# Query and key preparation inside the input projection, squares of each norm one stage earlier, setup and first adaptive vectors in one stage

## The reference, cut to what matters

```
for l in range(DEPTH):
    sh1, sc1, gt1, sh2, sc2, gt2 = adaln_vectors(cvec, W['ada_w'][l], W['ada_b'][l])
    h = modulate(rms_norm(x, W['norm1_w'][l]), sh1, sc1)
    # l == 0: even_mixer(h, ...); l == 1: odd_mixer(h, ...)
    x = x + gt1 * y
    h = modulate(rms_norm(x, W['norm2_w'][l]), sh2, sc2)
    x = x + gt2 * sq_relu_mlp(h, W['mlp_w1'][l], W['mlp_w2'][l])
```

```
qa, ka, va, qb, fa, fb, vb, gb = jnp.split(h @ w_in, offs, axis=-1)
qa = rms_norm(qa.reshape(bsz, n_tok, A_HEADS, HEAD_DIM), q_norm)
ka = rms_norm(ka.reshape(bsz, n_tok, A_KV_HEADS, HEAD_DIM), k_norm)
# latent tokens: qa, ka = apply_rope(...); then block_attention
q = jax.nn.silu(heads_b(qb, B_DK))
f_f = lb + (1 - lb) * jax.nn.sigmoid(heads_b(fa, B_DK))
o = rms_norm(o_f + o_b[:, ::-1], g_norm) * jax.nn.silu(heads_b(gb, B_DV))
```

## Time and profile before

| | us |
|---|---|
| median of 3 runs | 2501.28 (2498.02 to 2506.66) |
| profiled execution | 2492.64 |
| its span, first to last instruction | 2490.8 |
| PE busy | 2208.8 (89%) |
| DVE busy | 1125.0 (45%) |
| ACT busy | 839.3 (34%) |
| POOL busy | 279.0 (11%) |

### The profile page before, as it was taken

The page is one execution under the profiler, slowest core; times in us unless marked ns, Lnnn a source line. Parts: engine busy times, 40 slices in busy tenths (PEclk is TensorE's granted clock), DMA queues, the critical chain, the costliest instruction groups (busy, mean ns, idle before and its releaser), DMA issues. The chain is left out here.

```text
span 2490.8 us, 58690 instructions
## 1 busy us (share of the span) xinstructions
PE 2208.8 (89%) x26275; PEld 1882.8 (76%) x26275; DVE 1125.0 (45%) x2028; ACT 839.3 (34%) x1513; POOL 279.0 (11%) x526
## 2 busy tenths in 40 slices
PE   5999676879899999988996888888888789999999
PEld 2588354548799999974585677777776669999998
DVE  0311365533543244218133677777784354324421
ACT  3222355431421122126222565556653232111211
POOL 0000032100000000000000444343442000000000
PEclk9999798889899999999998899999998899999999
DMA  6110003881122222202110000000000212322221
GB/s 247 68 68 34 13 1 134 312 309 32 54 83 68 85 68 79 74 18 76 68 68 5 8 7 9 9 9 9 9 6 5 102 51 68 85 68 73 80 69 59
DMA packets 160742, 167.75 MB, mean 67 GB/s; under 512 B 13788, under 2 KB 117996, under 8 KB 160364
## 3 DMA queue, kind: packets, MB, share of 16 engines
q1 hardware_dynamic: 160492, 164.00, 20.4%
HBM read 160.44 MB, written 3.54 MB: 66 GB/s over the span
## 5 line engine op out<-in xcount | busy, mean ns | idle before, releaser
L168 PE MATMUL psum<-arena 64*64 64x64 f32 (+6 forms) x17072 | 828.9, 248 | 158.1 <-DVE arena L1033 17.7
L168 PEld LDWEIGHTS psum<-arena 64*64 64x64 f32 (+3 forms) x17072 | 664.2, 145 | 361.4 <-issue 170.3
L168 PE MATMUL psum<-norm_high,weights_high 128*128 128x320 f32 x1024 | 237.5, 313 | 16.6 <-DVE norm_low L532 16.4
L168 PE MATMUL psum<-norm_low,weights_high 128*128 128x320 f32 x1024 | 235.2, 311 | 0.0
L168 PE MATMUL psum<-norm_high,weights_low 128*128 128x320 f32 x1024 | 235.1, 311 | 0.0
L168 PE MATMUL psum<-hidden_low,weights_high 128*128 128x320 f32 x1024 | 233.5, 309 | 0.0
L168 PE MATMUL psum<-hidden_high,weights_high 128*128 128x320 f32 x1024 | 233.2, 309 | 0.0
L168 PE MATMUL psum<-hidden_high,weights_low 128*128 128x320 f32 x1024 | 233.2, 309 | 0.0
L585 ACT ACTIVATE weights_high<-weights 128x2048 fp32r<-128x2048 f32 x62 | 118.6, 1913 | 338.4 <-PE psum L168 338.4
L168 PEld LDWEIGHTS psum<-norm_high,weights_high 128*128 128x128 f32 x1024 | 172.2, 190 | 21.1 <-issue 10.8
L630 DVE SCALAR_TENSOR_TENSOR arena<-psum,ada,arena 128x320 f32<-128x320 f32 (+2 forms) x96 | 36.3, 434 | 314.5 <-PE psum L168 314.5
(11 more groups left out here) (200 smaller groups left out, 2765.3 us busy)
## 6 DMA issues: line engine op xcount, KB each, us to landing
weights<-in_mlp_w SPq DMA_DIRECT2D x64, 1024.0 KB, 5.6
arena<-in_ada_w SPq DMA_DIRECT2D x24, 2048.0 KB, 8.7
arena<-in_ab_w_in SPq DMA_DIRECT2D x6, 2048.0 KB, 7.7
arena<-in_ab_w_out SPq DMA_DIRECT2D x2, 2048.0 KB, 9.8
arena<-in_rwkv_wv SPq DMA_DIRECT2D x2, 2048.0 KB, 8.2
arena<-in_rwkv_wr SPq DMA_DIRECT2D x2, 2048.0 KB, 8.4
arena<-in_rwkv_wk SPq DMA_DIRECT2D x2, 2048.0 KB, 9.1
arena<-in_rwkv_wo SPq DMA_DIRECT2D x2, 2048.0 KB, 10.8
```

The source lines that it names most:

```text
L168: return nc.tensor.matmul(out, lhsT, rhs, start=start, stop=stop, skip_group_check=shared)
```

## The change

Four things are done.

1. Setup and the adaptive stage become one stage. SP loads the constants and x first, then the first adaptive block, then the twenty small arrays (`load_rows`), then the other blocks. PE turns four units of x, then the parameters, then the other four. ACT squares each unit of x for norm 0 as it is copied.
2. Each norm's squares are made in the stage ahead of it (`norm_square`), POOL adds up the first seven (`norm_pool`), and PE sums only that total and the eighth square, in four products where there were sixteen (`norm_pe`). The root (`norm_rms`) closes that stage. For norms 1 and 3 the multiplication of x by it moves from DVE to POOL (`norm_scale(pool, G, i)`); for 0 and 2 it stays on DVE.
3. The preparation of queries and keys is spread over the input projection: after the tiles 10 to 17 ACT, PE and DVE each do one piece (`qk_act`, `qk_pe`, `qk_norm_dve`, `qk_rope_dve`), key tile first. The QB tiles move behind the F tiles. The rotation tables and the cached keys are loaded after the second weight block.
4. The gates of HGRN are finished in the projection: for QB and GB ACT writes the sigmoid of the PSUM tile to scratch and DVE multiplies PSUM by it; for F DVE applies the lower bound. HGRN keeps only the logarithms.

```diff
-                                 (cols(w, 768, 512), 8, 512, cm_tiles(U_QB, 4)),
                                  (cols(w, 1280, 512), 8, 512, cm_tiles(U_F, 4)),
                                  (cols(w, 1792, 512), 8, 512, cm_tiles(U_F + 4, 4)),
+                                 (cols(w, 768, 512), 8, 512, cm_tiles(U_QB, 4)),
...
+        def norm_square(act, i, k, ready, count):
+            act.wait_ge(S(ready), count)
+            if k >= 2:
+                act.wait_ge(S("norm_squares_added"), 6 * i + max(1, k - 2))
+            A.activation(unit(NORM_AT[i][k % 2]), unit(U_X + k), ACT.Square).then_inc(S("norm_square"), 1)
+
+        def norm_pool(pool, i):
+            a0, a1, total = (unit(u) for u in NORM_AT[i])
+            for k in range(1, KT - 1):
+                pool.wait_ge(S("norm_square"), 8 * i + k + 1)
+                if k > 1:
+                    pool.wait_ge(S("norm_squares_added"), 6 * i + k - 1)
+                G.tensor_tensor(total, a0 if k == 1 else total, (a0, a1)[k % 2], ALU.add).then_inc(S("norm_squares_added"), 1)
+
+        def norm_rms(act, step, i):
+            log_exp_tables()
+            act.wait_ge(S("norm_sum"), i + 1)
+            r = unit(U_S + 2)
+            step(A.activation(r, pair(4), ACT.Ln, bias=EPSC[:, 0:1]))
+            A.activation(r, r, ACT.Exp, scale=-0.5).then_inc(S("norm_rms"), 1)
...
+        def norm_scale(eng, op, i):
             X = unit(U_X, 8)
-            dve.wait_ge(S("norm_rms"), i + 1)
+            eng.wait_ge(S("norm_rms"), i + 1)
             for k in range(KT):
                 if k >= 2:
-                    dve.wait_ge(S("norm_out"), 8 * i + k - 1)
-                V.tensor_tensor(unit(U_S + 3 + k % 2), X[:, k, :], unit(U_S + 2), ALU.mult).then_inc(S("norm_scaled"), 1)
-                if i % 2 and k:
-                    norm_split(dve, i, k - 1)
+                    eng.wait_ge(S("norm_out"), 8 * i + k - 1)
+                op.tensor_tensor(unit(U_S + 3 + k % 2), X[:, k, :], unit(U_S + 2), ALU.mult).then_inc(S("norm_scaled"), 1)
...
+            for n in range(n0 + 11, n0 + 31):
+                i, x = n - n0, tile_at("in", n)[2]
+                if i < 30:
+                    fast_low(dve, fast_of[n + 1])
+                if 11 <= i < 16:
+                    qk_norm_dve(dve, i - 11)
+                if 13 <= i < 18:
+                    qk_rope_dve(dve, step, i - 13)
+                if U_F <= x < U_F + 8:
+                    dve.wait_ge(S("tile_evacuated"), n + 1)
+                    p = (x - U_F) % 4
+                    V.tensor_scalar(unit(x), unit(x), LB[:, 5, p:p + 1], LB[:, 4, p:p + 1], ALU.mult, ALU.add)
+                elif i >= 23:
+                    dve.wait_ge(S("gate_sigmoid"), i - 22)
+                    V.tensor_tensor(unit(x), pair(2 * (n % 2)), unit(U_S + n % 2), ALU.mult).then_inc(S("tile_evacuated"), 1)
...
+        def qk_pe(pe, n):
+            i = n - first_tile["in"]
+            if 11 <= i < 16:
+                k = i - 11
+                pe.wait_ge(S("qk_square"), k + 1)
+                if k:
+                    pe.wait_ge(S("qk_rms"), k)
+                sq = unit(U_S + k % 2)
+                mm(PS[:, 4, 0:NS], bd64, sq[:, 0:NS])
+                mm(PS[:, 5, 0:NP_], bd64, sq[:, NS:T]).then_inc(S("qk_sum"), 1)
+            if 13 <= i < 18:
+                k = i - 13
+                pe.wait_ge(S("qk_normed"), k + 1)
+                if k:
+                    pe.wait_ge(S("qk_roped"), k)
+                mm(PS[:, 6, 0:NS], con(C_ROPE), unit(U_Q + QK_TILES[k])[:, 0:NS]).then_inc(S("qk_swapped"), 1)
...
             for p in range(4):
-                pool.wait_ge(S("hgrn_sig"), 2 * p + 2)
-                for j, u in enumerate((U_QB, U_GB)):
-                    G.tensor_tensor(unit(u + p), unit(u + p), HT[:, j, :], ALU.mult).then_inc(S("hgrn_gated"), 1)
...
+            load_input(sp)
+            load_blocks(sp, "ada0", lambda i: load_rows(sp) if i == 0 else None)
+            load_blocks(sp, "in", lambda i: qk_loads(sp) if i == 1 else None)
```

More of the change, by code:

```diff
@@ L271, in program, with products @@
                 b += 1
-        def products(pe, name, act, each=None, after=lambda i: None):
+        def products(pe, name, act, each=None, after=lambda n: None):
             n = first_tile[name]
@@ L602, in mlp_act @@
                     mlp_high(act, NBLK * l + n + 1, n + 1, l)
+                if l == 0 and half and kind == "down" and b:
+                    norm_square(act, 2, b - 1, "down_evacuated", 8 + b)
                 if kind == "up":
@@ L1092, in hgrn_dve @@
                     states(m + 1)
-                if i == 0 and p < 3:
-                    gates(p + 1)
                 if i == 1 and p < 3:
@@ L1162, in hgrn_act @@
                 if i == 0 and p < 3:
-                    sigmoids(p + 1)
+                    logs(p + 1)
                 if i == 2 and p < 3:
@@ L2287, in _ @@
             step = Steps(pool, "pool_step")
-            for i in range(4):
+            norm_pool(pool, 0)
+            for i in range(2):
                 stage_end(pool, "pool")
```

310 lines of the change are left out of this document (156 added, 154 removed).

## The result

| | before | after |
|---|---|---|
| median | 2499.65 (2495.99 to 2506.66, 4 runs) | 2439.61 (2436.8 to 2441.54, 4 runs) |
| profiled execution | 2492.64 | 2436.8 |
| its span | 2490.8 | 2435.0 |
| PE, DVE busy | 2208.8, 1125.0 | 2178.2, 1135.6 |
| ACT, POOL busy | 839.3, 279.0 | 828.0, 350.5 |

The ratio is 0.9756, with a 95% interval of 0.9731 to 0.9780: 60.0 us faster by the medians. The forecast was 2438. It lies 1.6 us from the measured median, yet the sum behind it did not hold term by term, as the ledger shows. A row of the ledger is the lead of the changed kernel at one event, the event's time before minus its time after.

A forecast was written before the change was run, and what follows sets the result against it. PE was busy 2208.8 of 2490.8 us, so only its idle stretches could shrink; terms of 61.5 plus 1 for attention gave 62.5 us off 2501.28, 2439, forecast as 2438, range 2416 to 2454.

The forecast's parts named there:

- Setup and norm 0: Program start to norm 0's first scaling: DVE scales right after the adaptive vectors; 15.9 us gained, ends 10 and 17.
- I put the first adaptive product at 25 where it was at 26.17: Start of the adaptive stage: x arrives earlier, so PE's first adaptive product gains 1 us, ends -4 and +2.
- rival (d): Start: parameters behind the first 2 MB block delay the adaptive stage; 5 to 6 us less, 2444; inside the forecast's 0.68.
- Input projection: Query and key preparation: 35.4 us gap goes, less moved PE work, tile 15's chain stall and tail; 21.4 us gained.
- (b): Input projection: DVE waits in order, tiles 11 to 17 each start about 2 us late; 14 us less gain, 2453; chance 0.14.
- (c): Input projection: waits between tiles bring a half-rate PE clock; through all 21 tiles 153 us cost, 2592; chance 0.03.
- Attention's start: Attention's first scores: they now follow a busy PE; one more us gained.
- HGRN: HGRN's opening and inside: logarithms start with the stage, steps shorten; 5.85 + 7.6 - 1.0 = 12.4 us, ends 8 and 14.
- I take 1.0 off: Inside HGRN: DMA of the 2 MB blocks is next in line as bound; 1.0 us deducted from the gain.
- Norm 2: Last update of x to norm 2's first scaling: 14.5 us become 4.0; 10.5 gained, ends 9 and 11.
- Norms 1 and 3: Those norms: roots gain 10.5 and 8.8, POOL and DVE excluding each other costs 18.0; 1.3 us gained, ends -3 and 23.5.
- Rival (a): Norms 1 and 3: POOL and DVE hardly disturb one another; total gain 84.7 us, time 2416.6; chance 0.14, in full or half.

The follow-up runs named there:

- the experiment: Against the changed kernel, PE takes adaptive block 0's products ahead of the last four units of x, SP's order unchanged; 2437.33 us, ratio 0.975.
- ACT's queue: Against the changed kernel, ACT's queue issues the twenty small loads, parameters and their SiLU go first, block 0's products ahead of x's last four units; 2435.86 us.
- half blocks: Against the changed kernel, only the first half of each of HGRN's twenty adaptive weight blocks is loaded, instructions the same; 2431.78 us, ratio 0.9726.

## Why the prediction was right, and where it wasn't

**Setup and norm 0, 15.9 forecast, 8.8 measured, under its own low end of 10.** The 14.9 us between vectors and scaling went as said. The step that failed is "I put the first adaptive product at 25 where it was at 26.17", with ends of -4 and +2. It came at 27.75, and what followed was worse: the adaptive stage ended 5.8 us later. I had named a cause in rival (d), parameters behind a 2 MB block, and priced it at 5 to 6 us, near the 7.1 that were missing; in the sum it stood at nothing. Two things were not in it. PE works through its program in order: block 0's products stood behind x, and the ring and the DMA engines behind block 0's products. Together with the late parameters this is behind the 3.4 us by which block 3's products were late; the order alone is worth 1.2 of them by the experiment. The other 2.4 us are the clock, 2.73 and 3.57 us for rows that had 1.92 and 1.95. Of the 3.7 us that the order on PE gave back, and the 7.5 with ACT's queue, 2.4 are this clock again, so the edits themselves are worth about 1.2 and 5.1.

**Input projection, 21.4 forecast, 22.2 measured.** The stall at the critical tile was 0.61 us (0.5 forecast), the tail 1.70 (1.7). The moved PE work was 212.0 - 200.5 - 0.6 = 10.9 us, not 11.8. Rivals (b) and (c) have nothing to show: PE has no other stall at tiles 11 to 17, and the clock stayed at 1.00.

**Attention's start, 1 forecast.** The first reduction is 32.1 us earlier where the first product is 31.0: 1.15 gained. Then the stage lost 2.0 us with the same instructions. In seven of the ten later kernels the stretch from first reduction to HGRN's first scores took 105.2 to 105.7 us, here 106.9. The traces settle where it went. For the same 640 products of this stretch PE was busy 71.2 us, 69.0 before, 69.4 to 69.7 in those seven and 71.1 to 71.2 in the other three; the mean granted clock over the stretch was 0.93 here and 0.95 before. So the 2.0 us are the clock; what sets it was not found.

**HGRN, 12.4 forecast, 9.1 measured.** The opening was 5.8 (5.85). The inside was 3.3 instead of 7.6 - 1.0. The chain's part was right: with half blocks the gain is 148.8 - 141.4 = 7.4. The mis-sized term is "I take 1.0 off" for DMA: it cost 4.2. It had been read from one wait of 0.80 us in the kernel before, whose longer steps hid the others; with the chain gone there are six.

**Norm 2, 10.5 forecast, 10.5 measured.**

**Norms 1 and 3, 1.3 forecast, 5.1 measured.** The choice between exclusion and none was right. The price was a little too high: 24.0 us for 25.8, so 1.8 us of the summed work is not in the distance. Rival (a) would have had 14.7. PE also made up about a microsecond of the first distance in norm 1, so the loss there was 6.3 and in norm 3 7.4, not 9.0.

**Elsewhere, 0 forecast, 1.0 measured** over the RWKV projections and RWKV.

**The whole.** Two terms, the start and HGRN's DMA, were 7.1 and 3.3 us too high, norms 1 and 3 3.8 too low. Attention's loss of 2.0 and the gains of 0.8 and 1.0 in the projection and the RWKV stages, the last within those stages' own spread, nearly cancel. That leaves 6.7 us too much gain in the profiled execution. The median hid most of it: I carried over the 8.6 us between profiled run and median of before to the kernel after, whose profiled run was 2.8 under its median. So 2438 met 2439.61 partly by luck; by the terms alone the forecast was 6.7 us too fast. The signs of the terms, and the sizes of the projection, HGRN's opening and norm 2, were not luck: the rows bear them out.

## What to carry to other kernels

Where an engine's step is given to POOL to run beside DVE, don't count the two as side by side when both read SBUF; here 25.8 us of summed work took 24.0, taking the step back was worth 6.6 us, and moving the weight block into the stage before another 6.8. In a ring of buffers, first find who frees the first slot and what stands ahead of it on its engine in program order; a load that is in time doesn't help a product that is queued behind other work (with the new order on PE the block was there and its products came 1.7 us later than before that edit). Before a few microseconds are put down to an edit, compare the lengths of the same PE rows in both traces, since at the start 2.4 of 3.7 us were the clock. Where a chain is taken out of a stage, price the next bound with all its repeats: one visible wait of 0.80 us became six.

## What was not expected of the hardware

The issue of a 48 KB load took SP 5.96 us, against 0.41 near the head of the program before; ahead of it 1.0 MB of constants, 2.5 MB of x and a 2 MB block had been issued. No run shows which of them held it.

A stage whose instructions don't change is not of one length. In ten kernels HGRN lasted 144.7 to 151.4 us, and the RWKV projections with RWKV 874.0 to 879.7; the start's adaptive blocks ran at granted clocks of 0.50 or 1.00 (1.2 or 2.4 GHz) in the same code. For attention and HGRN PE's busy time for the same products follows the clock, 69.4 to 71.2 us and 119.7 to 124.4. An edit that gains 3 us ahead of such a stage can't be judged by the total alone; the first time after the edit at which the lead can be read is the better measure, once the rows up to there are seen to have the same lengths.
